# Reloading each expert weight buffer after its own product, storing token rows once, and weighing expert outputs inside the passes

## The reference, cut to what matters

```python
gates = ...                       # per token: top group, then its 2 best of 4 experts, weights p_group * p_expert
hid = silu(t @ w_gate[e]) * (t @ w_up[e])          # 1024 -> 512, for each of 16 experts e
y   = sum over the token's 2 experts of gate_e * (hid @ w_down[e])
x   = x + g2 * y                                   # g2: one vector per request group (context, latent)
```

## Time and profile before

| | us |
|---|---|
| median of 3 runs | 1093.02 (1092.41 to 1094.48) |
| the profiled execution: its own time | 1093.68 |
| the profiled execution: span of instructions | 1091.8 |
| PE busy | 918.7 (84%) |
| ACT, DVE, POOL busy | 246.5, 221.0, 171.0 |
| DMA moved | 320.90 MB, 294 GB/s on average |

### The profile page before, as it was taken

How to read it: one execution, slowest core, us unless ns; L and a number is a source line. 1 busy time by engine, 2 the same in 40 slices (tenths; PEclk the granted TensorE clock), 3 DMA queues, 4 the chain that set the end, 5 groups by cost and what they waited for, 6 DMA issues and landing times.

```text
span 1091.8 us, 17259 instructions
## 1 busy us (share of the span) xinstructions
PE 918.7 (84%) x6701; PEld 509.4 (47%) x6702; DVE 221.0 (20%) x509; ACT 246.5 (23%) x451; POOL 171.0 (16%) x288
## 2 busy tenths in 40 slices
PE   2899999998999966998899997599749999878760
PEld 0455446654446443554455553374435555433420
DVE  1100455201644350010010000602511001000005
ACT  1111123221223131222122221420402222211212
POOL 2001002201001032211121211300112121111112
PEclk9899999999999987999999999699959999998995
DMA  9985464566342884999999994942664999999944
GB/s 379 373 267 207 156 233 156 203 231 233 132 143 85 357 305 175 406 421 418 418 426 420 415 420 197 410 200 77 247 244 154 379 405 424 419 417 424 422 188 170
DMA packets 69227, 320.90 MB, mean 294 GB/s; under 512 B 13252, under 2 KB 15588, under 8 KB 53952
## 3 DMA queue, kind: packets, MB, share of 16 engines
q1 hardware_dynamic: 54592, 290.75, 66.5%
q0 software_dynamic: 9856, 18.51, 4.8%
q10 hardware_dynamic: 4736, 11.01, 2.6%
HBM read 308.70 MB, written 20.53 MB: 302 GB/s over the span
## 4 chain that ended last, share of the span: by engine, by line
PE 38%; DMA 22%; DVE 2%; ACT 2%; SPq 2%; issue 2%; ACTq 0%; POOLq 0%; POOL 0%; DVEq 0%
PE ps L847 14%; DMA ring<-in_moe_w_down 10%; PE ps L854 9%; PE ps L746 7%; DMA deep<-in_moe_w_down 6%; DMA deep<-hrow,gi 2%; DMA hrow<-deep 2%; SPq L379 2%; PE ps L823 1%; DMA ring<-in_w_mod 1%; PE ps L783 1%; ACT deep L938 1%; PE ps L765 1%; DVE deep L1413 1%; PE ps L828 1%
## 5 line engine op out<-in xcount | busy, mean ns | idle before, releaser
L847 PE MATMUL ps<-ring,deep 128*64 128x256 f32 x1600 | 183.6, 387 | 12.9 <-DMA ring<-in_moe_w_up 9.3
L847 PEld LDWEIGHTS ps<-ring,deep 128*64 128x64 f32 x1600 | 120.2, 140 | 82.7 <-issue 16.6
L568 PE MATMUL ps<-deep,ring 128*128 128x384 f32 x384 | 129.2, 494 | 4.2 <-ACT deep L938 4.2
L1409 DVE TENSOR_TENSOR deep<-deep,ps 128x128 f32<-128x128 f32 x76 | 18.4, 284 | 452.7 <-PE ps L847 452.7
L854 PE MATMUL ps<-ring,deep 128*64 128x512 f32 x400 | 94.7, 617 | 8.3 <-DVE deep L1413 8.3
L568 PEld LDWEIGHTS ps<-deep,ring 128*128 128x128 f32 x384 | 72.7, 192 | 58.2 <-issue 10.0
L847 PE MATMUL ps<-deep 128*64 128x256 f32 x832 | 92.9, 380 | 6.9 <-DMA deep<-in_moe_w_up 5.5
L571 PE MATMUL ps<-ring,deep 128*128 128x512 f32 x192 | 88.6, 614 | 0.0
L746 PE MATMUL ps<-ring,deep 128*128 128x512 f32 x192 | 83.8, 594 | 1.4 <-ACT deep L1018 0.8
L847 PEld LDWEIGHTS ps<-deep 128*64 128x64 f32 x832 | 60.9, 137 | 42.7 <-DMA deep<-in_moe_w_up 6.9
L501 PE MATMUL ps<-ring,scond 128*32 128x512 f32 x384 | 50.4, 649 | 27.7 <-DMA ring<-in_w_mod 26.9
(11 more groups left out here) (162 smaller groups left out, 773.0 us busy)
## 6 DMA issues: line engine op xcount, KB each, us to landing
ring<-in_w_mod SPq DMA_DIRECT2D x24, 2048.0 KB, 12.1
ring<-in_moe_w_gate SPq DMA_DIRECT2D x22, 2048.0 KB, 22.9
ring<-in_moe_w_up SPq DMA_DIRECT2D x22, 2048.0 KB, 27.7
ring<-in_moe_w_down SPq DMA_DIRECT2D x22, 2048.0 KB, 32.8
ring<-in_hgrn_w_in SPq DMA_DIRECT2D x10, 2048.0 KB, 8.3
deep<-in_moe_w_gate SPq DMA_DIRECT2D x10, 2048.0 KB, 20.6
deep<-in_moe_w_up SPq DMA_DIRECT2D x10, 2048.0 KB, 25.0
deep<-in_moe_w_down SPq DMA_DIRECT2D x10, 2048.0 KB, 30.6
```

Source lines behind the costliest of these rows:

```text
L568: last = mm(bank[:, 0:T], W[:, k, b * P:(b + 1) * P], hT[:, k, :], start=(k == 0), stop=(k == KD - 1))
L847: last = mm(ps[g * SLOTS:(g + 1) * SLOTS, GU_BANK[j], 0:2 * P], xt[:, b, h * SLOTS:(h + 1) * SLOTS], slot3(S[j])[:, k, g * F // 2:(g + 1) ...
```

## The change

- SP's reloading: `used` is replaced by the pass count. SP reads `npass` itself, adds up the passes of the experts, and waits for `gate_mm`, `up_mm` and `y_mm` in turn; each of the three matrices is requested when its own product of the last pass is through.
- `hrow` holds each row once. A second table `rows_idx` gives the row to gather, `slots_idx` the place to scatter to.
- The first wait of u = 7 and 8 is for the first gather, no longer for the stored rows.
- Routing weights are computed ahead of the index tables. Two more sets of matrix products (6 matmul calls) bring them into slot order (`slot_w`). In each pass DVE makes `mix` = g2 of the context half x weight + g2 of the latent half x weight, and writes `ysb` = PSUM x `mix`; ACT's copy is gone.
- `combine` is one addition of the two choices and one to `x`; ACT's part is gone. g2 comes as two half vectors on 64 partitions each (`gate_half`, four DMAs of 128 KB for two of 512 KB).
- Piece 23 of `w_mod` goes to slot 6 and is requested when expert 14 is done, ahead of the read-back. ACT's first square of layer 1 waits until PE is through with it.

```diff
                     elif u == 7:
-                        sp.wait_ge(M[l]["hrow_out"], 16 * TT)
+                        sp.wait_ge(M[l]["gathered"], 16)
...
+                sp.wait_ge(npass_set, l + 1)
+                n = sp.alloc_register(f"sp_pass{l}")
+                sp.reg_mov(n, 0)
+
+                def next_set(e, free, par):
+
+                    windows = sp.value_load(npass[0:1, free], min_val=1, max_val=WIN)
+                    sp.reg_add(n, n, windows)
+                    passes = sp.snap(n, min_val=1, max_val=WIN * NE)
+                    sp.wait_ge(M[l]["gate_mm"], passes)
+                    unit(e, par, 0)
+                    sp.wait_ge(M[l]["up_mm"], passes)
+                    unit(e, par, 1)
+                    sp.wait_ge(M[l]["y_mm"], passes)
+                    unit(e, par, 2)
+
                 with sp.Fori(1, NE // 3) as i:
                     for par in range(3):
-                        sp.wait_ge(M[l]["used"], 3 * i + (par - 2))
-                        for j in range(3):
-                            unit(3 * i + par, par, j)
...
+                        next_set(3 * i + par, bass.ds(3 * i + (par - 3), 1), par)
...
             sp.wait_ge(M[0]["used"], NE - 2)
             for u in (20, 21, 22):
                 mod_load(u)
+            sp.wait_ge(M[0]["used"], NE - 1)
+            mod_load(23)
             expert_rows(0)
...
+                        if name == "a1" and t == 0:
+                            act.wait_ge(mod_mm, 24)
...
-                    act.dma_start(scratch["hrow"][l].rearrange("(t p) c n -> p t c n", p=P)[:, t],
-                                  hrow[:, t:t + 1, :].to_broadcast((P, 2, D))).then_inc(m["hrow_out"], 16)
+                    act.dma_start(scratch["hrow"][l].rearrange("(t p) n -> p t n", p=P)[:, t], hrow[:, t, :]
+                                  ).then_inc(m["hrow_out"], 16)
...
                 dve.wait_ge(m["weights"], 1)
+                step(V.tensor_tensor(wv[:].rearrange("p c t w -> p (c t) w"), wnd[:],
+                                     wgt[:].rearrange("p c t -> p (c t)").unsqueeze(2).to_broadcast((P, ct, WIN)), ALU.mult))
+                dve.wait_ge(m["idx_mm"], 1)
+                V.tensor_scalar(rows_idx[:], ps[:, 3, 0:NE * WIN], -0.25, c_("row"), ALU.mult, ALU.add)
+                V.tensor_scalar(slots_idx[:, 0:NE * WIN], ps[:, 3, 0:NE * WIN], -1.0, c_("base"), ALU.mult, ALU.add
+                                ).then_inc(m["idx_ready"], 1)
...
+                        V.tensor_copy(w_now[:], slot_w[:, :, bass.ds(e * WIN + w, 1)].rearrange("p g o -> p (g o)")
+                                      ).then_inc(m["w_now"], 1)
+                        dve.wait_ge(m["w_now"], k_)
+                        V.tensor_scalar(mix[:], gate_half[:, 0, :], w_now[:, 0:1], None, ALU.mult).then_inc(m["mix"], 1)
+                        dve.wait_ge(m["mix"], first)
+                        V.scalar_tensor_tensor(out=mix[:], in0=gate_half[:, 1, :], scalar=w_now[:, 1:2], in1=mix[:],
+                                               op0=ALU.mult, op1=ALU.add).then_inc(m["mix"], 1)
+                        dve.wait_ge(m["mix"], second)
                         dve.wait_ge(m["y_mm"], k_)
+                        dve.wait_ge(m["scattered"], 16 * k_ + 32)
+                        V.tensor_tensor(ysb, ps[:, Y_BANK, :], mix[:], ALU.mult).then_inc(m["y"], 1)
...
-                    step(V.scalar_tensor_tensor(out=a, in0=a, scalar=wgt[:, 0, t:t + 1], in1=b,
-                                                op0=ALU.mult, op1=ALU.add))
-                    step(V.tensor_tensor(a, a, gate_bc[:, 1, GROUP_OF[t], :], ALU.mult))
-                    V.tensor_tensor(x[:, t, :], x[:, t, :], a, ALU.add).then_inc(m["x_done"], 1)
+                    step(V.tensor_tensor(a, a, b, ALU.add))
+                    V.tensor_tensor(halves(x[:, t, :]), halves(x[:, t, :]), a, ALU.add).then_inc(m["x_done"], 1)
```

More of the change, by code:

```diff
@@ L57, in const_columns @@
     at, n = {}, 0
-    for name, w in [("ident", 128), ("upper", 128), ("ones", 128), ("iota", 128), ("rev_group", 4), ("rev_expert", 16), ("window", WIN), ("above", WIN), ("base", 1), ("value", 6), ("stack", NL),
+    for name, w in [("ident", 128), ("upper", 128), ("ones", 128), ("iota", 128), ("rev_group", 4), ("rev_expert", 16), ("window", WIN), ("above", WIN), ("base", 1), ("row", 1), ("value", 6), ("stack", NL),
                     ("minus_half", 4), ("pick", 4)]:
@@ L310, in program @@
             place("moe0", u, MOE_SLOTS[0][u % 9])
-        for phase, u, s in [("mod", 20, 2), ("mod", 21, 0), ("mod", 22, 1), ("mod", 23, 3), ("four", 0, 0), ("four", 1, 1)]:
+        for phase, u, s in [("mod", 20, 2), ("mod", 21, 0), ("mod", 22, 1), ("mod", 23, 6), ("four", 0, 0), ("four", 1, 1)]:
             place(phase, u, s)
@@ L328, in slot_mod @@
         def slot_mod(s):
-            return ring[:, s, :].rearrange("p (k n) -> p k n", k=2)
+            return slot(s).rearrange("p (k n) -> p k n", k=2)
         def in_cols(u):
@@ L819, in route @@
                 last.then_inc(m["idx_mm"], 1)
+                pe.wait_ge(m["slot_vals"], 1)
+                for g, tiles in enumerate([(0,), (1, 2)]):
+                    pairs = [(c, t) for t in tiles for c in range(2)]
+                    for n, (c, t) in enumerate(pairs):
+                        last = mm(ps[:, W_BANK, g * NE * WIN:(g + 1) * NE * WIN], pos_oh[:, c, t, :],
+                                  [sg, hid][c][:, t * NE * WIN:(t + 1) * NE * WIN],
+                                  start=(n == 0), stop=(n == len(pairs) - 1))
+                last.then_inc(m["slot_mm"], 1)
             def turn_tokens(m):
@@ L874, in expert @@
                             last = gate_up(1, k)
-                        last.then_inc(m["gate_up_mm"], 1)
+                        last.then_inc(m["up_mm"], 1)
                         pe.wait_ge(m["gathered"], 16 * k_ + 16)
@@ L1085, in experts @@
                         act.reg_add(n, n, 1)
-                        act.reg_add(half, half, 1)
-                        first = act.snap(half, min_val=1, max_val=2 * WIN * NE)
-                        act.reg_add(half, half, 1)
-                        second = act.snap(half, min_val=1, max_val=2 * WIN * NE)
                         k_ = act.snap(n, min_val=1, max_val=WIN * NE)
-                        act.wait_ge(m["gate_up_mm"], first)
+                        act.wait_ge(m["gate_mm"], k_)
                         A(sg[:, 0:2 * P], ps[:, GU_BANK[0], 0:2 * P], ACT.Silu).then_inc(m["silu"], 1)
@@ L1094, in experts @@
                         A(xt[:].rearrange("p b s -> p (b s)"), ps[:, XT_BANK, :], ACT.Copy).then_inc(m["xt"], 1)
-                        act.wait_ge(m["y_mm"], k_)
-                        act.wait_ge(m["scattered"], 16 * k_ + 32)
-                        A(ysb, ps[:, Y_BANK, :], ACT.Copy).then_inc(m["y"], 1)
-            def combine(l):
-                act.wait_ge(M[l]["weights"], 1)
-                for t in range(TT):
-                    act.wait_ge(yback[t], 16 * (l + 1))
-                    A(yall[:, t, 1, :], yall[:, t, 1, :], ACT.Copy, scale=wgt[:, 1, t:t + 1]
-                      ).then_inc(M[l]["second"], 1)
             act.dma_start(x[:, 0, :], io["x_prompt"].rearrange("b t n -> (b t) n")).then_inc(s_x, 16)
             act.dma_start(x[:, 1:3, :], io["x_sample"].rearrange("b (t p) n -> (b p) t n", p=P)).then_inc(s_x, 16)
-            act.dma_start(yall[:, 0], io["pos"]).then_inc(s_pos, 16)
+            act.dma_start(pos, io["pos"]).then_inc(s_pos, 16)
             act.wait_ge(s_cond, 32)
```

102 lines of the change are left out of this document (57 added, 45 removed).

## The result

The changed kernel takes 1059.08 us (median of 4 runs, 1058.09 to 1061.09), the kernel before beside it 1093.15: a ratio of 0.9689, 95% interval 0.9672 to 0.9706. It is faster by 34 us; 1053 was forecast, 1044 to 1067 as the range. The profiled execution took 1058.09, its span is 1056.22 (before 1091.84).

The account below looks back on a forecast made before the run. Layer 0 was taken as bound by PE with waits for weights, layer 1 by DMA at its end. Terms -7.4 - 7.6 - 6.7 - 16.3 - 5.0 = -43.0, with +0.2 and +2.4 -40.4, gave 1053 us; range 1044 to 1067.

Parts of the forecast that it names:

- The weighing is hidden: Each pass: DVE's added work, about 1.2 us, fits into the 3.5 us of the down product; uncovered, 1.2 a pass.
- 15 matrices of 5.4 us from 411.4: Layer 0: expert 7's gate, 15th from 411.4, lands at about 494.6, before PE wants it at 498.9.
- The end: End of the kernel: two DVE steps a tile instead of three, x done at 1075.45: -5.0 us, bounds -4 and -6.
- layer 0 to layer 1: Between the layers: piece 23 in time, the residual now late, PE turns at about 689.7: -6.7 us, bounds -3 and -8.
- a bound for the transition: Between the layers: only -3 us if DVE holds up POOL's steps for longer.
- The first gather: Start of each expert stage: rows stored once, gather on idle DMA takes 2.8 us, not 7.54: -7.4 us a layer.
- Reloading, layer 1: Layer 1: expert 5's set requested at about 856.0, not 872.30: -16.3 us, of which 7.4 is the earlier start.
- waits for gathers: Passes: POOL's index copy is delayed by DVE, 0.1 us for each of some 24 passes: +2.4, bounds 0 and +19.
- waits for weights: Layer 0: of 10.0 us, 7.6 go through earlier requests; expert 8's down stays late by some 2.4 us.
- layer 0 is bound by PE, with a tax: Layer 0 before the change: 18 passes take 223.7 us, unhindered 213.7; 10.0 us go to waits for weights.
- The 0 for the cold first pass: First pass of each layer, 2.46 us over a later one: no gain taken, bounds 0 and -2.5 per layer.
- The gather rival: Passes: the gather becomes the bound, +2.4 to +14.4 us in place of +2.4, 1056 to 1068, say 1062; chance 0.20.

Follow-up runs that it names:

- e1: Changed kernel, but SP asks for a whole set of three matrices only when its expert is done: 1072.77 us, ratio 0.9801 to the kernel before.
- e3: Changed kernel, but every token row is stored twice again, the second copy unread: 1064.30 us, ratio 0.9730 to the kernel before.
- e9: Changed kernel, but piece 23 of w_mod goes back to buffer 3 and behind the Fourier matrices in SP's queue: 1064.27 us, ratio 0.9719.
- e12: Changed kernel with the old amount of work in the sum of a token's two rows, values unchanged: 1066.35 us, ratio 0.9760 to the kernel before.
- e10: Kernel before with only the new request loop and its two semaphores for gate and up: 1076.85 us, ratio 0.9841 to the kernel before.
- e6: Changed kernel with a token's two rows side by side, read back as one 8 KB piece a partition: 1056.33 us, ratio 0.9652.
- e4: Changed kernel, but POOL copies the next pass's row numbers before it waits for the turn: 1057.51 us, ratio 0.9666 to the kernel before.
- e11: Changed kernel with packed rows (one 8 KB piece a partition) and the index copy ahead of the wait for the turn: 1054.15 us, ratio 0.9649.
- e2: Changed kernel, but matrices u = 7 and 8 wait for the stored rows again, not the first gather: 1061.67 us, ratio 0.9705.
- e5: Changed kernel, but DVE forms mix before the hidden products, away from POOL's index copy: 1058.80 us, ratio 0.9667 to the kernel before.
- e13: Changed kernel with 22 unread products filling PE's gap ahead of the turn of the Fourier input: 1062.88 us, ratio 0.9720.
- e14: Changed kernel with packed rows, index copy ahead, and unread products in PE's gaps at the Fourier turn and both routings: 1052.22 us, ratio 0.9618.

## Why the prediction was right, and where its terms were off

*The mechanism held.* In layer 0 the events that it named are where it put them: the first turn at 412.22 (forecast 411.4), expert 3's gate at 420.52 (420), no 0.00 in DMA's share from 424 to 432. Between the layers there is no wait for piece 23, and the turn comes 20.0 us behind the last down product (19). At the end there are two DVE steps a tile. In layer 1 the events are there but late: its first turn at 785.13 (778.5), its last matrix at 1021.53 (1014.7). e1, e3, e9 and e12 each take one part back and e10 puts one in alone, and each is worth about what its term said. The weighing is hidden, as forecast: in layer 0's passes PE waits 6.7 us for DVE's copy of the hidden rows, 6.6 before. Of the 4.8 us that are missing, 2.1 are at the end, 1.0 between the layers, 3.1 in the stretches to the two first turns and 0.5 ahead of them; layer 1's passes gave 1.9 more than forecast.

One figure on the way doesn't come out: 15 matrices of 5.4 us from 411.4 end at 492.4, not 494.6. Nothing hangs on it, as both lie before 498.9.

*The end, -5.0, measured -2.80, and layer 0 to layer 1, -6.7, measured -5.56.* The steps saved are worth about what I said (e12: +4.2 and +4.6). I had left two things out. I took the old landing times for the third tile; the new row layout, two pieces of 4 KB a partition, makes the read-back 1.4 us slower, and e6 gives back 1.4 and 1.5. And with fewer DVE steps POOL's norm steps are the chain at the end. Three of the five run beside two-input additions of DVE, two beside its last scaling, which also has two inputs. Those of line 1590 end some 0.05 us behind the DVE step, those of line 1593 some 0.4. They take up to 1.28 and 1.59 there, with medians of 0.19 and 0.56 over the run, and from `x` to the end it is 12.07 us, 0.7 more than before. I had put such a hold-up into a bound for the transition and not into the end.

*The first gather, -7.4 a layer: -7.14 in layer 0, -4.57 in layer 1.* The gather itself is nearly right in both: from the start of the first index table to the first turn it is 5.19 and 5.65 us, where it was 12.40 and 12.34, so -7.2 and -6.7. (It took 3.29 and 3.42 us; I took 2.8.) The 2.1 us that layer 1 lacks beyond this lie ahead of the table, at a lower clock: the Fourier input's turn takes 4.59 for 3.96, the first Fourier products 12.38 for 10.70. The first two rows are of the changed kernel, the third is of the kernel before.

```profile
407.03 0.32 DVE L1396 TENSOR_SCALAR rows_idx<-ps,const 128x96 uint32<-128x96 f32 x1 [0.49 <-PE ps L836]
...
779.48 0.32 DVE L1396 TENSOR_SCALAR rows_idx<-ps,const 128x96 uint32<-128x96 f32 x1 [0.50 <-PE ps L836]
```

```profile
795.30 0.32 DVE L1377 TENSOR_SCALAR slots_idx<-ps,const 128x96 uint32<-128x96 f32 x1 [1.53 <-PE ps L817]
```

In the runs that show 10.70 with nothing else moved between the Fourier turn and layer 1 (e4, e6, e11, e12) this stretch is 105.1 to 105.4, which is -5.9. Against these e2's 108.3 is the 3 us named above. The chain is 12.38 in e1, e5 and e10 too. In these four kernels the granted clock came up before the turn was through and fell again as the chain began; in the kernels with 10.70 it came up once and stayed, or never fell (e13). What decides this is not settled, and e14 shows that filling most of the gap is not enough.

*Reloading, layer 1.* Measured -10.31 for -8.4; 1.7 of it is the last down product, 3.67 us at a granted clock of 1.00, and 5.37 at 0.68 before. That is luck and not the reloading's: e5 and e6 reload in the same way and show 5.35 and 5.34. Without it the term is -8.6.

*Layer 0 came out at its forecast, -5.70, but not for its reason.* I added waits for gathers (+0.1 a pass, 1.9) to waits for weights (2.4). Both were there, 3.1 and 1.4, yet they aren't separate costs: when e4 took the 3.1 away, the waits for weights rose to 4.1. The timelines show why: the last wait for weights in layer 0 ends at a fixed time behind the request for u = 7, which begins the stream: 570.75 - 412.19 = 158.6 in the changed kernel, 158.7, 158.5 and 158.3 in e4, e11 and e14, and between these in e3, e5, e6, e9, e12 and e13. A pass that loses time to a gather before then only waits less for weights; one that gains it (e4, e5, and e14's first pass at full clock) waits more. The first row is of the changed kernel, the second of e14, where the request for u = 7 goes out at 411.52.

```profile
570.75 0.44 PE L856 MATMUL ps<-const,deep 128*128 128x128 f32 x2 [0.67 <-DMA deep<-in_moe_w_down]
```

```profile
569.81 0.44 PE L864 MATMUL ps<-const,deep 128*128 128x128 f32 x2 [1.10 <-DMA deep<-in_moe_w_down]
```

So the step that was wrong is to carry "layer 0 is bound by PE, with a tax" over to the changed kernel: the finer requests moved layer 0 to where the stream sets its passes up to 570 us. e2, whose stream begins 4.7 us earlier, has no such wait left and passes 2.9 us shorter. That is also why holding two matrices back bought 1.3 us there and not 4.7. The 0 for the cold first pass came out because it stayed cold (9.68 for 9.54); by e14 a warm one would have given layer 0 nothing either.

*The gather rival* had the hold-up right: the copy loses 0.3 us at the median (0.51 for 0.18) and 0.56 at most. The page SBUF — State Buffer of the Trainium skill (section Who interferes with whom) has the GpSimd step wait out the whole two-input step, and the copy that ends 0.05 us behind it agrees. Its price failed, because the stream covers the loss: with the copy free (e4) the passes of the two layers take 246.24 and 241.00 us, without 246.25 and 240.89.

## What to carry to other kernels

Where a stage alternates between two limits, don't add their waits: find the event to which the last wait of each kind is tied (here the first request of the stream), and price an edit by whether it moves that. When a buffer is laid out anew, price the transfers that read it, not only the steps that it saves; the two read-backs gave back 2.9 us. When work is taken off an engine at the end of a kernel, ask which chain was a step behind it: here it was POOL's, held by the two-input DVE steps that stayed.

The version with packed rows and the index copy ahead (e11) has a median of 1054.15, below the changed kernel's 1059.08, though the intervals of their ratios touch; the packing is what is shown to matter. With the gaps filled as well (e14, 1052.22) the intervals no longer touch.

## What was not expected of the hardware

- The read-back of the first 1 MB tile took 6.09 and 6.35 us in two 4 KB pieces a partition (changed kernel) and 4.67 to 4.83 in one of 8 KB (e6 and e11). Over all runs it is 6.09 to 7.02 and 4.67 to 5.02. SP was busy 1.84 to 1.88 us with the three requests in the first form, 1.28 to 1.29 in the second.
- Behind gaps of 11.96 to 12.13 us (changed kernel, e1, e5) the Fourier chain took 12.38 us, behind 12.24 and 12.34 (e4, e2) 10.70. With most of the gap filled and waits of 1.83 and 3.23 left it took 13.70 (e14); with all of it filled and one wait of 2.39 left, 10.70 (e13).
